# Moving the tiles that matmuls read to one residue of 2 KB, and the constants to the arena's end

## What is computed

```python
h = rms_norm(x, g_ffn1_pre)
x = x + 0.5 * rms_norm(swiglu(h, w_gate1, w_up1, w_down1), g_ffn1_post)
h = rms_norm(x, g_mix_pre)
q_sb, k_sb, v_sb, q_r, k_r, v_r, g_r, gate_sb, gate_ret = split(h @ w_in)
o_sb = stick_breaking_attention(q_sb, k_sb, v_sb)          # 8 heads x 64
o_r  = group_norm(retention(rotary(q_r), rotary(k_r), v_r)) * silu(g_r)   # 4 heads x 128
merged = sigmoid(gate_sb) * (o_sb @ w_proj_sb) + sigmoid(gate_ret) * (o_r @ w_proj_ret)
x = x + rms_norm(merged @ w_out, g_mix_post)
h = rms_norm(x, g_ffn2_pre)
x = x + 0.5 * rms_norm(swiglu(h, w_gate2, w_up2, w_down2), g_ffn2_post)
```

## The kernel before, in words

| tiles | remainder |
|---|---|
| `x_tok`, `h_hi`, `h_lo`, `w_raw`, `w_hi`, `w_lo`, `cst` | 128 |
| all that starts at `region` or `en`: `act`, `a_hi`, `a_lo`, `gate_s`, `xn`, `g_b`, `sp`, `cum`, `v_sb`, `v_r`, `qk_hi`, `qk_lo`, `qk_r`, `sig`, `tm`, `m_hi`, `m_lo` | 256 |
| `wt`, `gn_c`, `gn_t` (they lie behind `cum`, which is 4.5 KB) | 768 |
| `o_sb_hi`, `o_sb_lo`, `o_r_hi`, `o_r_lo` (from `oe`) | 2016 |

## Time and profile before

### The profile page before, as it was taken

The page is one execution under the profiler, slowest core; times in us unless marked ns, Lnnn a source line. Parts: engine busy times, 40 slices in busy tenths (PEclk is TensorE's granted clock), DMA queues, the critical chain, the costliest instruction groups (busy, mean ns, idle before and its releaser), DMA issues.

```text
span 1540.0 us, 17715 instructions
## 1 busy us (share of the span) xinstructions
PE 1510.2 (98%) x6688; PEld 1209.1 (79%) x6688; DVE 545.3 (35%) x606; ACT 483.4 (31%) x681; POOL 51.7 (3%) x116
## 2 busy tenths in 40 slices
PE   5999999999999999999999999999999999999998
PEld 5888888888888778666666888898888888888886
DVE  3332222223333363334435344452322222233334
ACT  4322121213222243445555323342221212132222
POOL 0000000000000000321230000000000000000000
PEclk9999999999999999999999999999999999999999
DMA  6333333333222313111111333343333333332221
GB/s 216 105 95 95 96 94 100 93 107 110 93 91 91 121 55 109 55 55 42 42 41 49 89 108 102 104 110 95 95 95 95 95 97 94 107 102 92 94 96 55
DMA packets 194321, 141.77 MB, mean 92 GB/s; under 512 B 4464, under 2 KB 180848, under 8 KB 194160
## 3 DMA queue, kind: packets, MB, share of 16 engines
q1 hardware_dynamic: 193280, 137.91, 29.9%
q10 hardware_dynamic: 1008, 3.41, 0.6%
HBM read 139.20 MB, written 2.10 MB: 92 GB/s over the span
## 4 chain that ended last, share of the span: by engine, by line
PE 94%; DVE 4%; ACT 1%; DMA 1%; issue 0%; ACTq 0%; DVEq 0%
PE ps L379 21%; PE ps L381 20%; PE ps L380 20%; PE ps L386 9%; PE ps L387 9%; PE ps L388 9%; PE ps L591 2%; PE ps L568 1%; DVE xn L985 1%; PE ps L555 1%; DVE ps L972 1%; PE ps L572 1%; DVE x_tok L975 1%; DVE w_lo L956 1%; PE ps L559 1%; DMA g_b<-g_ffn_pre 1%
## 5 line engine op out<-in xcount | busy, mean ns | idle before, releaser
L379 PE MATMUL ps<-h_hi,w_hi 128*128 128x512 f32 (+1 forms) x1376 | 534.8, 389 | 8.8 <-DVE w_lo L956 8.0
L956 DVE TENSOR_TENSOR w_lo<-w_raw,w_hi 128x1024 fp32r<-128x1024 f32 (+1 forms) x260 | 309.1, 1191 | 607.2 <-ACT w_hi L702 606.5
L380 PE MATMUL ps<-h_lo,w_hi 128*128 128x512 f32 (+1 forms) x1376 | 523.6, 381 | 0.0
L381 PE MATMUL ps<-h_hi,w_lo 128*128 128x512 f32 (+1 forms) x1376 | 523.6, 380 | 0.0
L702 ACT ACTIVATE w_hi<-w_raw 128x1024 fp32r<-128x1024 f32 (+1 forms) x260 | 259.8, 1028 | 254.0 <-PE ps L388 247.1
L379 PEld LDWEIGHTS ps<-h_hi,w_hi 128*128 128x128 f32 x1376 | 259.8, 189 | 72.8 <-issue 23.9
L380 PEld LDWEIGHTS ps<-h_lo,w_hi 128*128 128x128 f32 x1376 | 259.9, 189 | 50.4 <-issue 2.9
L381 PEld LDWEIGHTS ps<-h_hi,w_lo 128*128 128x128 f32 x1376 | 259.7, 189 | 49.1
L386 PE MATMUL ps<-w_hi,a_hi 128*128 128x512 f32 x512 | 202.5, 395 | 0.7 <-DVE a_lo L1010 0.7
L387 PE MATMUL ps<-w_lo,a_hi 128*128 128x512 f32 x512 | 202.2, 395 | 0.0
L388 PE MATMUL ps<-w_hi,a_lo 128*128 128x512 f32 x512 | 202.2, 395 | 0.0
(11 more groups left out here) (109 smaller groups left out, 871.9 us busy)
## 6 DMA issues: line engine op xcount, KB each, us to landing
w_raw<-w_ffn_gate SPq DMA_DIRECT2D x64, 512.0 KB, 4.0
w_raw<-w_ffn_up SPq DMA_DIRECT2D x64, 512.0 KB, 4.0
w_raw<-w_ffn_down SPq DMA_DIRECT2D x64, 512.0 KB, 3.3
w_raw<-w_in SPq DMA_DIRECT2D x44, 512.0 KB, 3.8
w_raw<-w_out SPq DMA_DIRECT2D x8, 512.0 KB, 5.3
w_raw<-w_proj_sb SPq DMA_DIRECT2D x8, 256.0 KB, 2.7
w_raw<-w_proj_ret SPq DMA_DIRECT2D x8, 256.0 KB, 2.6
out<-x_tok SPq DMA_DIRECT2D x3, 512.0 KB, 2.6
```

The lines of the kernel that those rows point to most:

```text
L379: pe.matmul(ps[:, bank, out_cols], wh, src_hi, start=first, stop=False)
L380: pe.matmul(ps[:, bank, out_cols], wh, src_lo, start=False, stop=False)
L381: return pe.matmul(ps[:, bank, out_cols], wl, src_hi, start=False, stop=last)
L956: dve.tensor_tensor(w_lo[:, slot, 0:cols], w_raw[:, slot, 0:cols], w_hi[:, slot, 0:cols].bitcast(F32), ALU.subtract).then_inc(w_lo_done, 1)
```

## The change

The diff moves tiles in the arena; no instruction is added, removed or reordered. `cst` and the three small tiles of the norms, which lay between the weights and the tables, go to the arena's end. `region` is thereby a multiple of 2048 in the arena. `cum` goes behind `gn_t`, and `oe` is rounded down to a multiple of 2048.

```diff
+CONST_BYTES = 2080
+LINE = 2048
...
+        small_at = ARENA - 3 * 32 - CONST_BYTES
+        cst, e = place("cst", [P, CONST_COLS], at=small_at)
+        ssq, e = place("ssq", [P, 2 * TT], at=e)
+        std, e = place("std", [P, 2 * TT], at=e)
+        rstd, e = place("rstd", [P, 2 * TT], at=e)
...
-        cst, _ = place("cst", [P, CONST_COLS])
-        ssq, _ = place("ssq", [P, 2 * TT])
-        std, _ = place("std", [P, 2 * TT])
-        rstd, _ = place("rstd", [P, 2 * TT])
         decay, _ = place("decay", [P, RH, T])
         rope, _ = place("rope", [P, 2, T])
         region = top[0]
+        assert region % LINE == 0
...
         sp, e3 = place("sp", [P, 3, T], at=region)
-        cum, e3 = place("cum", [P, 3, T - P], at=e3)
         wt, e3 = place("wt", [P, 4, T], at=e3)
         gn_c, e3 = place("gn_c", [P, T], at=e3)
         gn_t, e3 = place("gn_t", [P, T], at=e3)
+        cum, e3 = place("cum", [P, 3, T - P], at=e3)
...
-        oe = ARENA - 4 * PAIRS * T * 4
+        oe = (small_at - 4 * PAIRS * T * 4) // LINE * LINE
```

## The result

| | before | after |
|---|---|---|
| median of 6 runs, us | 1542.38 (1541.64 to 1542.83) | 1532.15 (1530.92 to 1532.78) |
| span of the profiled execution, us | 1540.0 | 1530.5 |

The ratio of the times is 0.9933, with a 95% interval of 0.9922 to 0.9944: the change takes 10.2 us away. The forecast was 1532.1.

The account below looks back on a forecast made before the run. PE, busy 98% of the span, was taken to bound the kernel through its matmul step. Savings of 10.35 us less 0.1 us of waiting give 10.25 us off the 1540.0 us span, 1529.75; forecast time 1532.1 us, range 1529 to 1543.

Parts of the forecast that it names:

- `a`: Down stages: 1464 matmuls on a_hi and a_lo, moved from remainder 256 to 128, each save 5.7 ns, 8.3 us.
- `m`: Out stage: 120 matmuls on m_hi and m_lo, moved from remainder 256 to 128, each save 5.7 ns, 0.7 us.
- `o`: Merge: 96 steps each on o_sb and o_r, moved from remainder 2016 to 128, save 1.35 us together.
- The steps at the end of down and out that lie beside a norm: 72 matmuls each of last_down (first block) and last_out, tiles 1 to 3: saving becomes a wait, counted as nothing.
- What PE saves there it waits: At the two norms: the chain gets no shorter and PE waits some 0.4 us more at each.
- The wait for the last weights: End of each down stage: PE's wait, 0.7 us together before, grows by 0.1 us for both.
- Constants and fills: Sums and heads: taken as nothing; bounds 1.0 us either way for constants, 1.7 less to 1.3 more for fills.
- Rival B: Whole kernel: placement is not the cause and nothing changes, 1542.3 us; chance 14%.
- B's variant: Arena starts 128 bytes past a 2 KB multiple, so partition addresses miss the aim; time stays if only remainder 0 helped.
- C: Sums: the constants' new place exposes 128 loads, up to 188 ns each, 24 us; slower, 1556 us; chance 5%.
- D: Down: the stream settles only partly, or DVE and ACT hold PE up; half the gain, 1537 us; chance 5%.
- E: Heads and sums: fills settle too, transposes and sums gain, 1.7 + 1.7 us more, 1528.7 us; chance 3%.

Follow-up runs that it names:

- `a` alone: Kernel before, with only the down stage's tiles a_hi and a_lo moved to remainder 128 (gate_s moves along): 1534.25 us, ratio 0.9945.
- the run without the three parts: Changed kernel with a, m, o_sb and o_r moved back to a difference from w, constants left at their new place: 1542.15 us, ratio 0.9999.
- The run with the weights' slots: Changed kernel with w_hi's four slots 0, 64, 128 and 256 bytes past the activations' remainder, w_lo's 256 more: 1546.8 us, single execution.
- the map: Three variants of the changed kernel, each slot of a_hi and a_lo at its own distance (4 to 512 bytes) from w's remainder: 1543.7, 1541.2, 1538.3 us.

## Why the prediction was right

The step of each stage decided, and the tile sorted the steps; that reading held for `a`, `m` and `o`, with the weights in either role. By its terms:

- `a`: 8.3 us were forecast. The two down stages gave 3.91 and 4.28 us, 8.2 together, and `a` alone 8.4 in the medians.
- `m`: 0.7 forecast, 0.69 found. `o`: 1.35 forecast, and the merge is 1.40 us shorter.
- The steps at the end of down and out that lie beside a norm were given no value, and gave none: from the norm's first instruction to the first fill it is 66.71 us before and 66.75 after. The chain still ends on DVE before PE, 1.19 us from the start of `h_lo` to PE in the rows after, as in the earlier trace rows:

```profile
558.61 1.14 DVE h_lo L997
...
559.80 0.50 PE ps L392
```

- What PE saves there it waits, some 0.4 us more at each norm, as was said. At the second norm it is in the row of `xn` in the view of PE's waits, first before, then after:

```profile
PE ps L401 <- DVE xn L985: 0.4, 1, 0.4
PE ps L407 <- DVE xn L991: 0.7, 1, 0.7
```

At the first, the rows of the waits are the same before and after; the time is between the last transpose of tile 1 and the first matmul of the values, whose starts are 0.03 us apart before and 0.37 after.

- The wait for the last weights was to grow by 0.1 us in sum. The row that answers to the earlier trace rows says 0.9 for 0.7 us, so 0.2 instead of 0.1:

```profile
PE ps L392 <- DVE a_lo L1016: 0.9, 2, 0.4
```

- Constants and fills at nothing: right, by the heads' 228.75 and 228.69 us and by the run without the three parts, 0.9999. The bounds around them were not needed. The argument for the constants was weaker than it looked: at 5.7 ns a matmul a pair of sums would pay 0.01 us, which is what the rows are read to. The run with the weights' slots shows it: there the matrix of minus ones and `sp` start at the same byte modulo 256, and its pair takes 0.96 us too (636.99 to 637.95), as do the pairs before and after, which lie 136 and 232 bytes apart modulo 256.

That the medians meet the forecast to 0.1 us is in part luck: the start alone differs by up to 1.5 us between the profiled executions, and the six runs of the changed kernel lie between 1530.92 and 1532.78. The stages, which differ from the forecast by at most 0.06 us each behind the start, say more. One reading was too broad: a 9 in the page's row of the clock stands for 90% and more, and in the first 38.5 us before the granted clock is 0.91 on the mean. In the windows from which the up and down steps come it is 1.00.

Rival B fell: `a` was moved down by 2176 bytes in the change and up by 1920 in the run with `a` alone, stays where it was in the memory at large, and its step falls to 226.7 both times. The rule that spoke for B stands in the Trainium skill (SBUF — State Buffer, Who interferes with whom): PE has two independent read ports and never waits on anyone. That the two ports are independent is not borne out here: where the stationary operand starts 4 bytes past the place at which the step is 226.7 ns, the step is 232.4. B's variant, that the change does not do what it says, was right as to the addresses (all tiles but the four small ones begin 128 bytes past a multiple of 2 KB) and wrong as to the time: remainder 0 gives nothing more. C did not happen. Neither did D, as the step is 226.7 through both down stages, nor E, as the fills stay at 230.

What the prediction left unsaid is the modulus: it took "128 on both sides" from the rows. They already ruled out 2 KB and 1 KB. The stationary slices of `product` are 512 bytes apart, so the up stage, at 226.7 throughout, holds differences of 0, 512, 1024 and 1536 bytes; `a` and `m`, 128 from `w`, rule out 128 and all that divides it. That leaves 512 and 256; which of the two, and that the rest of the change gives nothing, only the runs could tell.

## What to carry to other kernels

Where PE bounds a kernel, work out the distance from start to start of its matmuls in each stage, and compare stages of the same shape; the mean durations in the rows (389 to 390 ns and 395) hint at a difference, but what a matmul costs is in the starts (226.7 and 232.4). If the steps of float32r matmuls differ by stage, look at where the two operands begin: here they have to agree modulo 256 bytes, which some padding gives, while multiples of 2 KB and the constants' place gave nothing of their own. Try a rule on placement by one kernel that gives each slot of a ring its own distance: a single execution then holds four points of the map, though a unit's first and last steps still carry the price of the slots beside it.

## What the runs showed of the hardware that was not expected

- The step of a float32r matmul of 512 columns with its load of 128, in these streams at granted clock 1.00, is 226.7 ns if both operands start at the same byte modulo 256 (tried at 0 and at 128), and 229 to 234 ns for every other distance tried, from 4 bytes on; 192 bytes stand out with 229.2. The sign counts: a stationary operand 64 bytes past the moving one gives 233.3, one 64 bytes before it 229.6.
- The price is one of the stream, not of single matmuls: one operand of three at a distance of 128 bytes makes 231.9 ns of 226.7, and in the map a good unit behind a slow one has three to seven straying steps before it settles.
- The float32 sums of 512 columns pay nothing for it: 0.96 us a pair with the constants 136, 232 and 0 bytes from `sp` modulo 256 (before, after, and with the weights' slots moved).
